# Two transformer blocks: pair transfers behind their forms, and twelve seven-product slabs in the first feed forward

## The chip, the cores and the metric

One NeuronCore of one Trainium2 chip runs the whole kernel. The time is the device time of one execution in microseconds; the median of several runs is what counts. One more execution was taken with the profiler on, and all rows below come from it.

## The reference

256 tokens of width 1024, all in float32, go through two blocks. What matters here is the end of the first block, its feed forward:

```
u = rmsnorm(h, norm_ff_g) @ w1          # 1024 -> 4096
h = h + square(relu(u)) @ w2            # 4096 -> 1024
```

The first block has in front of it a mixer (`w_in`, softmax attention with forget gates, a gated recurrence, `w_out`) and cross attention over 256 memory tokens. The second block (differential attention, pooling, memory attention, gates, a convolved feed forward) follows it. The kernel computes float32 products in three passes of TensorE: each operand is split into a high part (`hi`, fp32r) and the remainder (`lo`), and `mm3` issues hi x hi, hi x lo and lo x hi.

## The kernel before

**Slabs.** All weights stream through a ring of three buffers (`RING = 3`) as slabs of up to 128 x 2048 elements, numbered through the whole kernel in the order of use. SyncE (SP) loads slab n into `raw` (`load`) once the low part of slab n-3 has been made. ScalarE makes `whi` (`hi`), once slab n-3 has left TensorE. VectorE makes `wlo` (`lo`), and TensorE multiplies.

**First feed forward.** `w1` is cut in 16 up slabs `u0` to `u15` (256 hidden columns each), `w2` in 16 down slabs (256 hidden rows each). `FIRST_FFN` is the order, written out by hand: `u` is an up slab, `n` a plain down slab (8 block products of 128 x 128 with 512 columns, 24 matmuls), and `s` a down slab by seven products of blocks (Strassen and Winograd's scheme, 21 matmuls). HIDS = 7 places hold the split hidden activations between an up slab and its down slab.

**What a seven-product slab needs.** Three of its seven products use blocks of the slab as loaded; four use forms T1 to T4, sums and differences of blocks:

- T1 and T3 are made by transfers. SP loads two blocks of the upper half into `pairs` (`pair`, line 523), and GpSimd then adds the other two by an accumulating DMA into the same place (`add_blocks`, line 738). `pairs` has two buffers, `forms_hi`/`forms_lo` one (`FORMS = 1`).
- The three blocks that are used as they are (in `raw`; in the text, "the forms of n" on SP) come by two transfers: line 534 (512 KB) and line 535 (256 KB).
- T2 and T4 are made by VectorE in `rest` (`weight_sums`, lines 2440 and 2441), which waits for the accumulate's semaphore `sev["acc0"]` or `sev["acc1"]`.
- ScalarE makes `forms_hi` (`form_hi`, line 1825) and VectorE `forms_lo` (`form_lo`, line 2448), each in two halves; `sev["lo"]` counts the halves. TensorE waits for the first half after nine matmuls and for the second after fifteen (`seven_slab`).
- The hidden side needs sums too: `hidden_sums` (lines 2417 to 2420, tile `sq`) before `hid_hi` (line 1813) and `hid_lo` (line 2426).

**Order on VectorE.** For position n of the order: `hidden_sums` if it is an up slab for a seven-product slab; `form_lo` twice for a slab whose forms buffer comes free with n; `lo(n + 3)`; `weight_sums(n + 3)` if that is a seven-product slab; `hidden_lo`. ScalarE goes the same way with `relu_square`, `form_hi`, `hi(n + 3)`, `hidden_hi`. `split_after` says at which position a slab's forms are split: when slab n-3 is done or the seven-product slab before it, whichever is later.

**Pair transfers before.** `load(n)` issues, right behind slab n's own transfer, the pair of slab n+2 if that is a seven-product slab. It counts on the semaphore of slab n (`raw_landed`), so ScalarE's `hi(n)` waits for it as well. From the third pair on, SP waits first until the first half of `forms_lo` of the slab two seven-product slabs back is made, since the buffer is used again. `add_blocks` on GpSimd waits for slab n-2's semaphore.

Of the kernel before, what the change touches and what calls it, by code (L numbers as in the profile page):

```python
# [35 lines left out]
RING = 3  # L36
HIDS = 7
FORMS = 1
SQUARES = 2
FIRST_FFN = "u0 u1 u2 u3 u4 u5 u6 s0 u7 s1 u8 s2 u9 s3 u10 s4 u11 s5 u12 s6 u13 s8 u14 s10 u15 n7 s12 n9 s14 n11 n13 n15"  # L40
SLAB = 2048
NEG = -1e30
EPS = 1e-6
# [7 lines left out]
def ffn_order():  # L51

    return [(step[0], int(step[1:])) for step in FIRST_FFN.split()]

# [69 lines left out]
def two_blocks(nc, w, out):  # L124
# [4 lines left out]
    slabs, first = plan(w)  # L129
# [13 lines left out]
    SEVEN = [n0 + i for i, (kind, j) in enumerate(ORDER) if kind == "s"]  # L143
# [2 lines left out]

    landed = [0] * NS
    for n in range(NS):
        landed[n] = (landed[n - RING] if n >= RING else 0) + (32 if n in SEVEN or n >= first["cv"] else 16) + 16 * (n + 2 in SEVEN)

    with ExitStack() as ctx:
        def sem(name):
            return ctx.enter_context(nc.semaphore(name))

        def sb(name, shape, dt=F32, at=None):
            return (at or ctx).enter_context(nc.sbuf_tensor(name, shape, dt))

        def sems(prefix, names):
            return {n: sem(f"{prefix}_{n}") for n in names.split()}
# [55 lines left out]
        with ExitStack() as r3:  # L215
# [4 lines left out]
            pairs = sb("pairs", [P, 2, 2, 512], at=r3)  # L220
# [48 lines left out]
        raw_landed = [sem(f"raw_landed{i}") for i in range(RING)]  # L269
# [8 lines left out]
        lam_in, bias_in, mem_in = (sem(n) for n in "lam_in bias_in mem_in".split())  # L278
# [26 lines left out]
        sev = sems("sev", "acc0 acc1 t hi lo kept")  # L305
# [59 lines left out]
        def slab(t, n, nk):  # L365
            return t[:, n % RING, :nk * slabs[n][3]].rearrange("p (k c) -> p k c", k=nk)
# [73 lines left out]
        def quarter(t, q, order=QUARTERS):  # L440
            tt, c = order[q]
            return t[:, tt, c * 512:c * 512 + 512]
# [27 lines left out]
            return out  # L470

        EARLY = SEVEN[0] - first["w1"]

        def up_bank(j):

            return tb[:, j - 1, :] if j in (2, 3, 4) else acc[:, 0, 0, :] if j == 5 else acc[:, 1, 1, :]
# [5 lines left out]
        held, places, before = {}, {}, {}  # L482
# [22 lines left out]
        def raw_forms(n):  # L505
            return raw[:, n % RING, :].rearrange("p (s c) -> p s c", c=512)
# [7 lines left out]
        @block.sync  # L514
        def _(sp):
            def pair(n):

                if n + 2 not in SEVEN:
                    return
                i = SEVEN.index(n + 2)  # L520
                if i >= 2:
                    sp.wait_ge(sev["lo"], 2 * i - 3)
                sp.dma_start(pairs[:, i % 2, :, :], slabs[n + 2][1][:, :, 512:1024]).then_inc(raw_landed[n % RING], 16)

            def load(n, src=None, wait=None):
                if n >= RING:

                    sp.wait_ge(lo_ready, n - RING + 1 if wait is None else wait)
                if n - RING in SEVEN:
                    sp.wait_ge(sev["t"], SEVEN.index(n - RING) + 1)  # L530
                _, ap, nk, c, _ = slabs[n]
                if n in SEVEN:
                    forms = raw_forms(n)
                    sp.dma_start(forms[:, 1:3, :], ap[:, :, 0:512]).then_inc(raw_landed[n % RING], 16)
                    sp.dma_start(forms[:, 3, :], ap[:, 1, 512:1024]).then_inc(raw_landed[n % RING], 16)
                    pair(n)
                    return
                dst, src = slab(raw, n, nk), ap if src is None else src
                if n < first["cv"]:
                    sp.dma_start(dst, src).then_inc(raw_landed[n % RING], 16)  # L540
                    pair(n)
                    return

                for part in range(2):
                    if len(src.shape) == 4:
                        d, s = dst[:, :, part * P:part * P + P], src[:, :, part, :]
                    else:
                        d, s = dst[:, part, :], src[:, part, :]
                    sp.dma_start(d, s).then_inc(raw_landed[n % RING], 16)

            def loop(name, src, iters):

                n0 = first[name]
                with sp.Fori(0, iters) as i:
                    for u in range(RING):
                        load(n0 + u, src(i, u), i * RING + (n0 + u - RING + 1))

            def load_x(q):
                t, c = QUARTERS[q]
                sp.dma_start(quarter(h, q), w["x"][t * P:t * P + P, c * 512:c * 512 + 512]).then_inc(x_in[q], 16)  # L560

            def load_piece(n, p):

                _, ap, nk, _, _ = slabs[n]
                if n >= RING and p == 0:
                    sp.wait_ge(lo_ready, n - RING + 1)
                w = nk // PIECES[n]
                k = slice(p * w, p * w + w)
                landed_at = raw_landed[n % RING] if p == PIECES[n] - 1 else piece_in[n % RING, p]
                sp.dma_start(slab(raw, n, nk)[:, k, :], ap[:, k, :]).then_inc(landed_at, 16)  # L570

            for g in range(4):
                sp.dma_start(turned_x[:, 2 * g:2 * g + 2, :], w["xT"][:, 2 * g:2 * g + 2, :]).then_inc(xT_in[g], 16)
                load_piece(0, g)
                load_piece(1, g)
            for p in range(PIECES[2]):
                load_piece(2, p)
            for q in range(4):
                load_x(q)
            for p in range(PIECES[RING]):  # L580
                load_piece(RING, p)
            sp.dma_start(cols[:, 16:NC0 + NCW], w["cols"][:, 16:NC0 + NCW]).then_inc(cols_in["rest"], 16)
            sp.dma_start(small[0:8, 59:60], w["fox_f_bias"].rearrange("a h -> h a"),
                         allow_slow_non_contiguous=True).then_inc(bias_in, 16)
            for i, n in enumerate(("lambda_q1_2", "lambda_k1_2", "lambda_q2_2", "lambda_k2_2")):
                sp.dma_start(fpt[:, 0, 64 * i:64 * i + 64], w[n].broadcast_to([P, 64])).then_inc(lam_in, 16)
            for n in range(RING + 1, first["cv"]):
                if n in PIECES:
                    for p in range(PIECES[n]):
                        load_piece(n, p)  # L590
                else:
                    load(n)
            upv = w["w_up_2"].rearrange("(k p) (two c) -> p k two c", p=P, two=2)
            loop("cv", lambda i, u: upv[:, :, :, bass.ds(i * 384 + u * 128, 128)], 7)
            for n in range(first["cv"] + 21, NS):
                load(n)
# [3 lines left out]
        def _(pool):  # L600
# [79 lines left out]
            for m in range(1, 8):  # L680

                half = 1 << (m - 1)
                n = P // (2 * half)
# [48 lines left out]
            def add_blocks(n):  # L732

                i = SEVEN.index(n)
                pool.wait_ge(raw_landed[(n - 2) % RING], landed[n - 2])
                if i >= 2:
                    pool.wait_ge(sev["lo"], 2 * i - 3)
                pool.dma_start(pairs[:, i % 2, :, :], slabs[n][1][:, 0, :].rearrange("p (a c) -> p a c", a=2),  # L738
                               accum_op=ALU.add).then_inc(sev[f"acc{i % 2}"], 16)

            add_blocks(SEVEN[0])
            square_scale()

            pool.dma_start(xn[:, 1, :], w["final_norm_g"].rearrange("(a c) -> a c", a=1).broadcast_to([P, D])
                           ).then_inc(gfin_in, 16)
            for n in SEVEN[1:]:
                add_blocks(n)
# [19 lines left out]
            for g, win in enumerate(POOL_W):  # L767
# [5 lines left out]
                n = win - 1  # L773
# [2034 lines left out]
```

## Time and profile before

| | us |
|---|---|
| median of 3 runs | 883.44 (882.94 to 883.51) |
| profiled execution | 884.5 |
| its span | 882.8 |
| TensorE busy | 872.9 (99%) |
| VectorE busy | 648.7 (73%) |
| ScalarE busy | 521.2 (59%) |
| granted TensorE clock | 0.999 |

The span is what the profiler shows from the first to the last instruction; the rest of the profiled execution's time lies around it. The first feed forward lies between about 269 and 443 us of the span. In the page and the views, PE is TensorE, DVE is VectorE, ACT is ScalarE, POOL is GpSimd and SP is SyncE; `L798` is a line of the kernel. Matmuls overlap in the pipeline, so the distance between two starts says more than the duration shown.

### The profile page before, as it was taken

Reading aid. Unit: us, or ns where it says so; the run is one execution under the profiler, and the core shown is the slowest. Engines: PE = TensorE matmul, PEld = TensorE weight load, DVE = VectorE, ACT = ScalarE, POOL = GpSimd, SP = SyncE. Lnnn points to the kernel's source line nnn. Section 1 sums busy time; section 2 is a strip of 40 time slices with the busy share of each in tenths; the row PEclk is TensorE's granted clock in tenths of the full one; section 3 lists DMA queues with packets and bytes.
Section 4 is the critical chain, followed back from the end, with each engine's and each line's share of the span. In section 5 each row is a group of like instructions: output and inputs, shape, how many; then the busy total and the mean of one; then the engine's idle time right before and its main releaser. Section 6 shows DMA issues by size and latency. Waiting matters only on the chain.

```text
span 882.8 us, 15682 instructions
## 1 busy us (share of the span) xinstructions
PE 872.9 (99%) x6254; PEld 806.4 (91%) x6254; DVE 648.7 (73%) x887; ACT 521.2 (59%) x761; POOL 127.8 (14%) x147
## 2 busy tenths in 40 slices
PE   9999999999999999999999999999999999999997
PEld 9998988989989998888899989999998899999886
DVE  5887987757538888897875548988686788888643
ACT  6786655546547766675573356656634766666432
POOL 5561333000000100000142250001000100000000
PEclk9999999999999999999999999999999999999999
DMA  9969544354535989998656554354556387676541
GB/s 296 319 232 299 178 144 144 97 174 150 176 92 183 254 239 261 268 296 268 203 175 220 192 186 141 106 190 137 174 192 191 104 226 195 194 196 204 192 143 48
DMA packets 141932, 169.42 MB, mean 192 GB/s; under 512 B 4592, under 2 KB 114288, under 8 KB 141616
## 3 DMA queue, kind: packets, MB, share of 16 engines
q1 hardware_dynamic: 138224, 155.72, 55.0%
q0 software_dynamic: 2928, 11.80, 5.5%
q8 instruction: 43, 0.70, 0.4%
q10 hardware_dynamic: 720, 1.06, 0.3%
q14 instruction: 17, 0.14, 0.1%
HBM read 167.51 MB, written 1.05 MB: 191 GB/s over the span
## 4 chain that ended last, share of the span: by engine, by line
PE 85%; DVE 5%; DMA 4%; issue 3%; ACT 2%; SPq 0%; POOL 0%; DVEq 0%; POOLq 0%; ACTq 0%
PE tb L798 15%; PE tb L800 15%; PE tb L799 15%; PE acc L798 10%; PE acc L800 10%; PE acc L799 10%; DMA pairs<-in_w 3%; DMA raw<-in_w_in 1%; PE acc L1140 1%; DVE forms_lo L2448 1%; ACT whi L1487 1%; DVE hid_lo L2426 1%; DVE wlo L2054 1%; DVE rest L2440 1%; DVE wlo L2127 1%
## 5 line engine op out<-in xcount | busy, mean ns | idle before, releaser
L2054 DVE TENSOR_TENSOR wlo<-raw,whi 128x2048 fp32r<-128x2048 f32 (+1 forms) x138 | 310.4, 2254 | 126.2 <-ACT whi L1487 125.5
L1487 ACT ACTIVATE whi<-raw 128x2048 fp32r<-128x2048 f32 (+1 forms) x138 | 259.3, 1880 | 151.7 <-PE acc L800 79.3
L798 PE MATMUL tb<-xhi,whi 128*128 128x256 f32 x1000 | 278.7, 279 | 0.8 <-DVE wlo L2127 0.5
L799 PE MATMUL tb<-xlo,whi 128*128 128x256 f32 x1000 | 276.4, 276 | 0.0
L800 PE MATMUL tb<-xhi,wlo 128*128 128x256 f32 x1000 | 276.3, 276 | 0.0
L798 PEld LDWEIGHTS tb<-xhi,whi 128*128 128x128 f32 x1000 | 187.9, 188 | 1.9 <-issue 1.8
L799 PEld LDWEIGHTS tb<-xlo,whi 128*128 128x128 f32 x1000 | 187.9, 188 | 0.1
L800 PEld LDWEIGHTS tb<-xhi,wlo 128*128 128x128 f32 x1000 | 187.9, 188 | 0.0
L798 PE MATMUL acc<-xhi,whi 128*128 128x256 f32 x256 | 71.4, 279 | 1.0 <-DVE wlo L2054 1.0
L799 PE MATMUL acc<-xlo,whi 128*128 128x256 f32 x256 | 70.8, 277 | 0.0
L800 PE MATMUL acc<-xhi,wlo 128*128 128x256 f32 x256 | 70.8, 276 | 0.0
L798 PEld LDWEIGHTS acc<-xhi,whi 128*128 128x128 f32 x256 | 48.1, 188 | 2.9 <-issue 2.8
L799 PEld LDWEIGHTS acc<-xlo,whi 128*128 128x128 f32 x256 | 48.1, 188 | 0.2
L800 PEld LDWEIGHTS acc<-xhi,wlo 128*128 128x128 f32 x256 | 48.1, 188 | 0.0
L800 PE MATMUL acc<-whi,xlo 128*128 128x512 f32 x112 | 44.0, 393 | 0.0
L798 PE MATMUL acc<-whi,xhi 128*128 128x512 f32 x112 | 43.9, 392 | 0.0
L799 PE MATMUL acc<-wlo,xhi 128*128 128x512 f32 x112 | 43.8, 391 | 0.0
L2003 ACT ACTIVATE cy<-tb,cols 128x256 f32<-128x256 f32 x44 | 22.5, 561 | 33.1 <-PE tb L800 33.1
L791 POOL TENSOR_TENSOR rs<-rs,half_neg 128x1 f32<-128x1 f32 x6 | 3.3, 554 | 266.7 <-DVE rs L2665 266.7
L738 POOL DMA_DIRECT2D pairs<-in_w x11 | 9.6, 877 | 170.9 <-DMA pairs<-in_w 170.9
L799 PE MATMUL acc<-wlo,vhi 128*128 128x512 f32 x88 | 34.2, 389 | 0.0
L798 PE MATMUL acc<-whi,vhi 128*128 128x512 f32 x88 | 34.2, 389 | 0.0
(435 smaller groups left out, 1737.9 us busy)
## 6 DMA issues: line engine op xcount, KB each, us to landing
raw<-in_w_in SPq DMA_DIRECT2D x37, 1024.0 KB, 5.3
raw<-in_w_up SPq DMA_DIRECT2D x44, 512.0 KB, 5.0
raw<-in_w SPq DMA_DIRECT2D x21, 1024.0 KB, 6.5
raw<-in_w_down SPq DMA_DIRECT2D x22, 512.0 KB, 4.1
raw<-in_w_xkv SPq DMA_DIRECT2D x8, 1024.0 KB, 5.6
raw<-in_w_out SPq DMA_DIRECT2D x8, 1024.0 KB, 4.9
pairs<-in_w SPq DMA_DIRECT2D x11, 512.0 KB, 4.9
pairs<-in_w POOLq DMA_DIRECT2D x11, 512.0 KB, 7.9
```

The lines of the kernel that those rows point to most:

```text
L738: pool.dma_start(pairs[:, i % 2, :, :], slabs[n][1][:, 0, :].rearrange("p (a c) -> p a c", a=2), accum_op=ALU.add).then_inc(sev[f"acc{i % ...
L798: pe.matmul(o, a_hi, b_hi, start=start, stop=False)
L799: pe.matmul(o, a_hi, b_lo, start=False, stop=False)
L800: return pe.matmul(o, a_lo, b_hi, start=False, stop=stop)
L1140: last = pe.matmul(acc[:, 1, t, i * 64:i * 64 + 64], a[:, s], lvl_view(b[:, s], m)[:, :, 1, :], start=True, stop=True)
L1487: act.activation(whi[:, n % RING, cut], raw[:, n % RING, cut], ACT.Copy).then_inc(hi_ready, 1)
L2003: last = act.activation(cy[:, b, g, :], tb[:, b, g * T:g * T + T], ACT.Identity, scale=cols[:, bass.ds(j + a, 1)], bias=cols[:, bass.ds(j ...
L2054: dve.tensor_tensor(low(n)[:, cut], raw[:, n % RING, cut], whi[:, n % RING, cut].bitcast(F32), ALU.subtract).then_inc(lo_ready, 1)
L2127: dve.tensor_tensor(low(n)[:, cut], raw[:, n % RING, cut], whi[:, n % RING, cut].bitcast(F32), ALU.subtract)\
L2426: dve.tensor_tensor(hid_lo[:, cut], sq[:, j % SQUARES, 0:cut.stop - cut.start], hid_hi[:, cut].bitcast(F32), ALU.subtract).then_inc(ffn["l ...
L2440: link(dve.tensor_tensor(t2, t1, b22, ALU.add))
L2448: dve.tensor_tensor(forms_lo[:, i % FORMS, cut, :], src, forms_hi[:, i % FORMS, cut, :].bitcast(F32), ALU.subtract).then_inc(sev["lo"], 1)
```

## The change

- `PAIR_IN`: the pair transfers count on two semaphores of their own, `lam_in` for even and `bias_in` for odd ones (both have been used once at the start of the kernel, up to 64 and 16). `landed` no longer counts them, and `hi` no longer waits for them.
- `pair(n)` is now issued for slab n itself, behind its two form transfers, and no longer with slab n-2.
- `add_blocks(n)` waits for the pair's own semaphore, and no longer for `sev["lo"]`.
- `FIRST_FFN`: the seven-product slabs are 0 to 10 and 12 (before: 0 to 6, 8, 10, 12, 14), the plain ones 11, 13, 14 and 15 (before: 7, 9, 11, 13, 15). `s9` and `s10` stand side by side, and `n13 n14 n15` are the last three.

```diff
-FIRST_FFN = "u0 u1 u2 u3 u4 u5 u6 s0 u7 s1 u8 s2 u9 s3 u10 s4 u11 s5 u12 s6 u13 s8 u14 s10 u15 n7 s12 n9 s14 n11 n13 n15"
+FIRST_FFN = "u0 u1 u2 u3 u4 u5 u6 s0 u7 s1 u8 s2 u9 s3 u10 s4 u11 s5 u12 s6 u13 s7 u14 s8 u15 s9 s10 n11 s12 n13 n14 n15"
@@ plan of the landings
-        landed[n] = (landed[n - RING] if n >= RING else 0) + (32 if n in SEVEN or n >= first["cv"] else 16) + 16 * (n + 2 in SEVEN)
+        landed[n] = (landed[n - RING] if n >= RING else 0) + (32 if n in SEVEN or n >= first["cv"] else 16)
@@
+        PAIR_IN = ((lam_in, 64), (bias_in, 16))
@@ SP
             def pair(n):
 
-                if n + 2 not in SEVEN:
-                    return
-                i = SEVEN.index(n + 2)
+                i = SEVEN.index(n)
                 if i >= 2:
                     sp.wait_ge(sev["lo"], 2 * i - 3)
-                sp.dma_start(pairs[:, i % 2, :, :], slabs[n + 2][1][:, :, 512:1024]).then_inc(raw_landed[n % RING], 16)
+                sp.dma_start(pairs[:, i % 2, :, :], slabs[n][1][:, :, 512:1024]).then_inc(PAIR_IN[i % 2][0], 16)
@@ SP, load(n)
                 if n < first["cv"]:
                     sp.dma_start(dst, src).then_inc(raw_landed[n % RING], 16)
-                    pair(n)
                     return
@@ GpSimd
             def add_blocks(n):
 
                 i = SEVEN.index(n)
-                pool.wait_ge(raw_landed[(n - 2) % RING], landed[n - 2])
-                if i >= 2:
-                    pool.wait_ge(sev["lo"], 2 * i - 3)
+                landing, before = PAIR_IN[i % 2]
+                pool.wait_ge(landing, before + 16 + 16 * (i // 2))
                 pool.dma_start(pairs[:, i % 2, :, :], slabs[n][1][:, 0, :].rearrange("p (a c) -> p a c", a=2),
                                accum_op=ALU.add).then_inc(sev[f"acc{i % 2}"], 16)
```

## Rows read from the trace of the kernel before

**Rows 1.** The page's first part: busy time, share of the span, instructions.

```profile
PE 872.9 (99%) x6254; PEld 806.4 (91%) x6254; DVE 648.7 (73%) x887; ACT 521.2 (59%) x761; POOL 127.8 (14%) x147
```

**Rows 2.** Windows between starts of seven-product slabs: length, busy PE, PEld, DVE, ACT, POOL.

```profile
308.31:318.56 10.25, 10.25 (x72) 9.41 (x70) 10.08 (x13) 7.91 (x8) 0.86 (x1) 1.00 0.91 241
...
360.02:371.85 11.83, 10.82 (x72) 9.29 (x71) 9.67 (x9) 7.39 (x8) 0.86 (x1) 1.00 0.85 243
...
sum 95.24, PE 93.61 PEld 84.17 DVE 79.80 ACT 63.81 POOL 7.78; mean PE 10.40 PEld 9.35 DVE 8.87 ACT 7.09 POOL 0.86
```

**Rows 3.** Waits from 265 to 445 us: total, times, longest.

```profile
ACT whi L1487 <- DMA pairs<-in_w: 16.5, 7, 3.1
...
PEld tb L798 <- DVE forms_lo L2448: 1.3, 2, 1.0
PE acc L798 <- DVE wlo L2054: 1.0, 3, 0.4
```

**Rows 4.** Chain that ended last, one stretch: start, us, what.

```profile
362.82 3.85 DMA pairs<-in_w
366.69 1.50 ACT whi L1487
```

**Rows 5.** Timeline of TensorE, first matmuls of slabs: start, duration.

```profile
313.09 0.28 PE L798 MATMUL acc<-xhi,whi 128*128 128x256 f32 x1
...
398.07 0.28 PE L798 MATMUL acc<-xhi,whi 128*128 128x256 f32 x1
...
403.55 0.39 PE L798 MATMUL acc<-whi,hid_hi 128*128 128x512 f32 x1
...
423.96 0.39 PE L798 MATMUL acc<-whi,hid_hi 128*128 128x512 f32 x1
```

**Rows 6.** Timeline of VectorE, one cycle.

```profile
332.98 0.28 DVE L2417 TENSOR_TENSOR sq<-sq 128x128 f32<-128x128 f32 x1
...
335.37 1.76 DVE L2054 TENSOR_TENSOR wlo<-raw,whi 128x1536 fp32r<-128x1536 f32 x1 [1.24 <-ACT whi L1487]
337.04 0.68 DVE L2440 TENSOR_TENSOR rest<-pairs,raw 128x512 f32<-128x512 f32 x1
337.76 0.69 DVE L2441 TENSOR_TENSOR rest<-rest,raw 128x512 f32<-128x512 f32 x1
338.37 1.08 DVE L2426 TENSOR_TENSOR hid_lo<-sq,hid_hi 128x896 fp32r<-128x896 f32 x1
339.49 1.23 DVE L2448 TENSOR_TENSOR forms_lo<-pairs,forms_hi 128x1024 fp32r<-128x1024 f32 x1
340.63 1.22 DVE L2448 TENSOR_TENSOR forms_lo<-rest,forms_hi 128x1024 fp32r<-128x1024 f32 x1
341.77 2.28 DVE L2054 TENSOR_TENSOR wlo<-raw,whi 128x2048 fp32r<-128x2048 f32 x1
```

**Rows 7.** Timeline of SP's issues: start, duration.

```profile
289.56 0.55 SPq L523 DMA_DIRECT2D pairs<-in_w  x1
...
333.10 0.37 SPq L534 DMA_DIRECT2D raw<-in_w  x1
333.51 0.47 SPq L535 DMA_DIRECT2D raw<-in_w  x1
```

**Rows 8.** Line 523, the pair transfers: issue durations in ns, landing in us.

```profile
L523 SPq DMA_DIRECT2D pairs<-in_w x11: 367/368/789, 278.1 to 392.5; - x11
...
DMA to landing us min/median/max: 3.7/4.9/8.5
```

**Rows 9.** Line 535, the 256 KB transfer behind the 512 KB one.

```profile
L535 SPq DMA_DIRECT2D raw<-in_w x11: 458/468/1904, 287.6 to 399.6; - x11
...
DMA to landing us min/median/max: 5.5/6.8/9.8
```

**Rows 10.** Line 738, the accumulating transfers of GpSimd.

```profile
L738 POOL DMA_DIRECT2D pairs<-in_w x11: 863/865/965, 286.5 to 400.9; - x11
...
DMA to landing us min/median/max: 6.9/7.9/9.5
```

## The prediction

> **What bounds the kernel now.** I read the page's busy shares first: TensorE is busy for 99% of the span [rows 1], so a change counts only by what it takes from TensorE's stream or by the time that it makes TensorE wait. Then the windows, cut at the starts of the first feed forward's seven-product slabs. Nine cycles of one seven-product slab and one up slab take 95.24 us; the undisturbed ones take 10.25 us, the worst 11.83 [rows 2]. Nine times 10.25 is 92.25, so TensorE loses 3.0 us there. The third reading is the list of waits in the stage: TensorE waits for `forms_lo` and `wlo`, which VectorE makes, and ScalarE waits 16.5 us, in seven waits, for the DMA of `pairs` before it may split a slab [rows 3]. The chain of waits shows this as a closed circle: pair DMA issued at 362.82, split by ScalarE at 366.69 [rows 4]; the sums, the low halves and the next pair DMA follow. So the stage is paced by a loop through the pair transfer, just above TensorE's own pace. The slab that waits is the one loaded together with the pair, two slabs ahead of the pair's own user, because both count on one semaphore.
>
> **TensorE's own work.** The window from 308.31 is cut by the first up product at 313.09 [rows 2, 5]: a seven-product slab (21 matmuls) takes 4.78 us, an up slab 5.47. A plain slab has 24 matmuls, by the same pitch 24 x 4.78 / 21 = 5.46. Twelve seven-product slabs in place of eleven save 0.68 us of the stream.
>
> **VectorE's work for it.** Slabs 7 and 9 become seven-product slabs, 14 no longer is one: each gives or takes four `sq` operations like the one of 0.28 us (1.2 with their gaps, the next work in the queue starts no sooner) and a `hid_lo` of seven blocks for one of four (1.08 x 3/7 = 0.4), 1.6 us in all [rows 6], plus forms and sums for one slab net. A cycle with all of it fits: the first window holds 10.08 us of VectorE work and TensorE still kept 10.25 [rows 2, 6]. I cost that at nothing as long as no wait is put in VectorE's queue; the bounds are nothing and the 1.6 us of each of the two, since VectorE has no more than 0.2 us to spare in such a cycle.
>
> **The transfers, which decide.** Removed: ScalarE's wait on the pair of two slabs ahead (up to the 3.0 us above come back), and SP's wait for `sev["lo"]` in front of the up slab's load. Under the new order that wait is met before it is reached, since `pair(n)` now stands behind the forms of slab n itself. Added: the pair's lead over its user shrinks by two slabs. For seven-product slab n the order is now:
>
> 1. SP issues the forms of n when `wlo` of slab n-3, an up slab, is done. Two issues at 333.10 and 333.51 with 0.47 us for the second [rows 7]: the pair goes out 0.9 us later. That assumes that nothing holds the issue.
> 2. The pair lands. The trace has no pair that follows its forms at the usual distance. Bounds: 3.7 us (a pair alone ahead in the queue) and 8.5 (the slowest one) [rows 8]. The nearest row is that of the 256 KB forms transfer, which stands at the end of SP's pair of form transfers: 5.5 / 6.8 / 9.8 us [rows 9]. I take 6.8.
> 3. GpSimd sees it and issues the accumulating DMA: 0.3 us from the wake-up, my estimate from GpSimd's issue lying a little behind ScalarE's start on the same landing. It lands after 6.9 / 7.9 / 9.5 us [rows 10]. I take 7.9.
> 4. VectorE, whose queue stands at `weight_sums(n)` until then, does both `rest` sums, `hid_lo`, `forms_lo` twice and `wlo` of the up slab n+1: from 337.04 to 341.77 + 2.28 = 344.05, that is 7.0 us [rows 6].
> 5. The end of that `wlo` is what releases the forms of slab n+4.
>
> This is a loop over four slabs, that is over two cycles: 0.9 + 6.8 + 0.3 + 7.9 + 7.0 = 22.9 us. TensorE needs 2 x 10.25 = 20.5. So the loop binds: 11.45 us per cycle. It binds as soon as pair and accumulate together take over 20.5 - 8.2 = 12.3 us; I have 14.7.
>
> The Trainium skill has a rule that bears on step 2 (DMA: Bandwidth & Descriptors, section "Queues, rings and completion order"): each DMA engine takes its descriptors in ring order within a queue and takes turns between queues. By it a pair behind 768 KB of forms lands after them and shares the engines with GpSimd's transfer. The spread of the pair's landings here, 3.7 to 8.5 us, fits this but doesn't show the order; my sum does not use it.
>
> **Start of the stage.** The pair of the first seven-product slab goes out behind its forms at 288.1 to 289.6 (L523 issues at 289.56 there now, for the next pair) instead of 278.1 [rows 7, 8]. With 7 to 8 us for the pair and 7.9 for the accumulate its sum is ready at 303.5 to 306. Behind it in VectorE's queue stand the sums (1.35), `hid_lo` (1.1), both `forms_lo` (2.3), four `sq` operations (1.2) and then `wlo` of the up slab (2.2) that TensorE wants at 313.09: 8.15 us [rows 6]. With the middle, 305, that is 313.1, no loss; the bounds are 0 and 1.1 us. From there VectorE has no lead, and each `wlo` of an up slab starts that slab.
>
> From the up slab 7 at 313.1 to up slab 15 there are eight cycles, four turns of the loop: 4 x 22.9 = 91.6, so slab 15 starts at 404.7. Before, it starts at 398.07 [rows 5]. **Loss: 6.6 us** (the 3.0 that come back are inside this difference).
>
> **The adjacent slabs.** There is one buffer of forms, so forms of s10 can be split only when s9 has ended. TensorE has nine matmuls of s10 that need none, 9 x 0.228 = 2.05 us; ScalarE (1.05) and VectorE (1.2) need 2.3 to 2.4. That alone is a stall of 0.3 us. But VectorE is late. The forms of s9 follow `wlo` of slab 14, which belongs to the other turn of the loop. That one starts with `wlo` of slab 8: behind 313.1 come `hid_lo`, four `sq`, `wlo` of a seven-product slab (1.7), sums, `hid_lo`, both `forms_lo` and `wlo`, 11.0 us, so 324.1, and three turns later 392.8. Plus 0.9 + 6.8 + 0.3 + 7.9, s9's accumulate lands at 408.7, sums and `hid_lo` to 410.7, both `forms_lo` to 413.0, `wlo` of s10 to 414.7. It then stands at the sums of s10, whose pair waited for the first `forms_lo` of s8 (404.7 - 7.0 + 1.35 + 1.1 + 1.15 = 401.3) and so lands with 6.8 + 0.3 + 7.9 at 416.3. Sums to 417.7, `wlo` of n11 to 419.9, `hid_lo` of slab 15 to 420.6, first `forms_lo` of s10 to 421.7. TensorE: slab 15 from 404.7 to 410.2, s9 to 415.0, the nine matmuls to 417.05. **Stall: 4.65 us.** Bounds 0.3 and 6. The rest (n11, s12, n13, n14, n15) has its splits in time by the same counting, as the plain slabs before have (no stall after 403.55), and the fold and residual are unchanged.
>
> **Sum.** 6.6 + 4.65 - 0.68 = 10.6 us. Before, n11 starts at 423.96; the slab that takes its place (n13) should start near 434.6. The profiled execution took 884.5 us with a span of 882.8; 1.7 us lie around it. The median of the runs is 883.44, 1.1 under the profiled one. I add the difference to the median: 894.0 us.
>
> **Rivals.**
>
> A, forecast: the loop through pair and accumulate binds. Between loops of 21.8 (pair 5.7) and 24.5 (both some 0.8 longer) and a stall of s10 of 2.5 to 6: 888 to 900 us. Chance 0.60.
>
> B, the landings get shorter when the pair's burst is spread out, pair 5.2 with 7.9: loop 21.3, as much as now (4 x 21.3 = 85.2 against 84.98), and VectorE instead of the transfers is what paces the rest. Stall of s10 some 2: 883.44 + 0.2 + 2 - 0.7 = 884.9. For it: half of the pair transfers before land within 4.9 us [rows 8]. Against: these lead their burst in the queue. Chance 0.15, from 883 to 888.
>
> C, the other side: pair and accumulate take under 12.3 us together, TensorE has its own pace. Then the 3.0 us come back, 0.68 are saved, and s10 costs 0.3 to 1: 880.2. One mechanism, decided at 12.3; the lowest rows (3.7 and 6.9) would allow it, the medians behind other transfers (6.8 and 7.9) speak against it. Chance 0.17. The skill's fit in the same page, section "Anatomy of one DMA — SWDGE (gpsimd) path", about 2 us plus bytes over 436 GB/s, would give 3.2 us for 512 KB, both together 6.4, and hence this result; no accumulate here landed under 6.9 [rows 10], so the trace speaks against it.
>
> D, both at their long ends through contention (8.5 and 9.5): loop 26.2, 4 x 26.2 = 104.8, a loss of 20 and 5 at s10: 907. Slower cycles thin the traffic, which speaks against it. Chance 0.08.
>
> **Chances.** What a measurement can tell from no change is 0.2%, 1.8 us. Faster by more: nearly all of C, 0.16. Within: the bottom of B and the edge of C, 0.08. Slower: 0.76. Range 881 to 900; the forecast's own is 888 to 900.
>
> **What the profile after would show.** Right: VectorE's idle time stands before `rest` L2440, released by the DMA of `pairs`; ScalarE's wait of `whi` on `pairs` is gone; windows between up slabs 7 and 15 come in twos of about 23 us; accumulate issues 7 us behind their pair; TensorE has one stall of 3 to 5 us in front of a `forms_hi` product near the end. Wrong: `rest` waits for nothing, cycles of 10.25 to 10.3, the 3.0 us gone; or a pair landing under 5 us behind its forms. If the stage is slower and `rest` waits for no DMA, VectorE's own work was mis-sized.

## The result, and the profile after

| | before | after |
|---|---|---|
| median, us (22 runs each) | 883.71 | 887.04 |
| lowest to highest | 881.51 to 886.35 | 882.83 to 889.41 |
| span of the profiled execution | 882.8 | 885.0 |

The ratio is 1.0033, interval 1.0024 to 1.0042: the change makes the kernel slower by 3.3 us. The forecast was 894.0, slower by 10.6. The direction was right, the size was wrong by a factor of three. The profiled span grew by 2.2 us; the parts below are counted against that.

TensorE's line of the page, where [rows 1] stands for before:

```profile
PE 873.0 (99%) x6251; PEld 807.1 (91%) x6251; DVE 652.6 (74%) x895; ACT 523.2 (59%) x763; POOL 125.0 (14%) x148
```

Three matmuls fewer, as counted. The windows of the stage, cut at the starts of seven-product slabs and around the late stalls; columns as in [rows 2], the third number from the end is the granted clock:

```profile
307.88:318.13 10.25, 10.25 (x71) 9.42 (x70) 9.89 (x12) 7.91 (x8) 0.85 (x1) 1.00 0.88 251
...
379.61:390.42 10.81, 10.52 (x72) 9.32 (x70) 9.59 (x9) 7.94 (x9) 0.85 (x1) 1.00 0.96 275
390.42:400.66 10.24, 10.24 (x71) 9.41 (x70) 5.57 (x4) 4.50 (x5) 1.71 (x2) 1.00 0.94 260
400.66:404.87 4.21, 2.22 (x11) 1.51 (x9) 3.26 (x5) 2.88 (x3) 0.00 (x0) 1.00 0.89 207
...
405.90:409.08 3.18, 3.18 (x8) 2.46 (x8) 3.15 (x5) 3.02 (x4) 0.00 (x0) 0.50 0.77 258
409.08:413.07 3.99, 2.48 (x12) 1.69 (x10) 3.96 (x4) 3.38 (x3) 0.86 (x1) 1.00 0.68 211
```

Of the nine cycles up to s9, eight take 10.24 or 10.25 us and one 10.81. From 307.88 to 400.66 are 92.8 us, against 95.2 before. What the change loses against before lies behind 400.66, in s9 and s10. The waits between 265 and 447 us (total, times, longest), where [rows 3] stands for before:

```profile
ACT forms_hi L1822 <- DMA pairs<-in_w: 27.8, 10, 6.6
DVE rest L2437 <- DMA pairs<-in_w: 16.1, 10, 5.3
...
PEld tb L795 <- DVE forms_lo L2445: 4.4, 2, 2.4
...
PE acc L795 <- DVE wlo L2051: 0.3, 1, 0.3
```

ScalarE's wait of `whi` on `pairs` is gone. VectorE's `rest` now waits for the accumulate in ten of twelve slabs. Both are signs that the forecast named for being right. But the cycles of 10.25 us and the 3.0 us gone are signs that it named for being wrong. One turn of the loop in the timelines of SP, GpSimd and VectorE (start, duration):

```profile
331.19 0.37 SPq L533 DMA_DIRECT2D raw<-in_w  x1
...
332.11 0.43 SPq L522 DMA_DIRECT2D pairs<-in_w  x1
...
352.39 0.37 SPq L533 DMA_DIRECT2D raw<-in_w  x1
```

```profile
338.46 0.85 POOL L735 DMA_DIRECT2D pairs<-in_w  x1 [10.01 <-DMA pairs<-in_w]
```

```profile
345.35 0.69 DVE L2437 TENSOR_TENSOR rest<-pairs,raw 128x512 f32<-128x512 f32 x1 [0.80 <-DMA pairs<-in_w]
...
350.08 2.28 DVE L2051 TENSOR_TENSOR wlo<-raw,whi 128x2048 fp32r<-128x2048 f32 x1
```

Forms issued at 331.19, pair 0.9 later, accumulate issued 6.35 after the pair, `rest` 6.9 after that, `wlo` ends at 352.36, and SP issues the forms four slabs further at 352.39: 21.2 us, against the 22.9 of the forecast and TensorE's 20.5. Landings of the pair on SP (the view of the tile `pairs`, SP alone) and of the accumulate (line 735), min / median / max, beside [rows 8] and [rows 10]. The trace tells the landing of only six of the twelve pairs; over all twelve, the accumulate's issue stands 4.8 to 8.6 us behind the pair's, 6.15 in the median.

```profile
DMA to landing us min/median/max: 5.3/6.1/8.3
```

```profile
L735 POOL DMA_DIRECT2D pairs<-in_w x12: 846/855/959, 294.4 to 409.6; - x12
...
DMA to landing us min/median/max: 5.5/7.3/9.5
```

How far VectorE is ahead of TensorE: the `wlo` of the up slabs 7 and 15, and the first matmul of each:

```profile
307.33 2.28 DVE L2051 TENSOR_TENSOR wlo<-raw,whi 128x2048 fp32r<-128x2048 f32 x1
...
391.95 2.29 DVE L2051 TENSOR_TENSOR wlo<-raw,whi 128x2048 fp32r<-128x2048 f32 x1
```

```profile
312.66 0.28 PE L795 MATMUL acc<-xhi,whi 128*128 128x256 f32 x1
...
395.19 0.28 PE L795 MATMUL acc<-xhi,whi 128*128 128x256 f32 x1
```

The end of the stage in the chain that ended last (start, length, what):

```profile
369.51 8.20 DMA pairs<-in_w
377.73 0.70 DVE rest L2437
...
382.54 2.21 DVE wlo L2051
...
385.74 5.95 DMA pairs<-in_w
...
391.98 9.54 DMA pairs<-in_w
401.54 0.70 DVE rest L2437
...
411.79 1.24 DVE forms_lo L2445
413.07 0.50 PE tb L795
```

This is the loop itself, closed through the split that releases the load: s7's accumulate (8.2 us), `wlo`, s9's pair (6.0), s9's accumulate (9.5). TensorE at the same place, and the first product of n13:

```profile
404.87 0.50 PE L795 MATMUL tb<-forms_hi,hid_hi 128*128 128x512 f32 x1 [1.99 <-DVE forms_lo L2445]
...
405.69 0.63 PE L795 MATMUL tb<-forms_hi,hid_hi 128*128 128x512 f32 x1
406.12 0.63 PE L796 MATMUL tb<-forms_lo,hid_hi 128*128 128x512 f32 x1
...
426.12 0.39 PE L795 MATMUL acc<-whi,hid_hi 128*128 128x512 f32 x1
```

s9 waits 2.15 us beyond the usual pitch for its first form (2.38 between two starts). Then the matmuls stand 0.43 us apart where 0.23 is usual, from 405.69 to 409.08, while the granted clock is 0.50, which is 1.2 instead of 2.4 GHz: eight steps in 3.39 us, 1.6 us lost. s10 waits 1.67 more. With 0.5 in the cycle of 379.61 that is 5.9 us lost (6.1 with the first matmul behind each stall, which takes 0.1 longer); regained are the 3.0 of the loop before and the 0.68. The difference is 2.2 to 2.4, as n13's start says (426.12 against 423.96 for the slab in that place, [rows 5]).

### The profile page after: what moved, and what is told of

The parts are those of the page before. It is cut to its first block, busy times and chain, and to the rows that moved or that the text cites. A ratio compares the mean times of both kernels' runs of the same rounds, so it can differ in the third digit from the quotient of the medians.

```text
span 885.0 us, 15677 instructions
## 1 busy us (share of the span) xinstructions
PE 873.0 (99%) x6251; PEld 807.1 (91%) x6251; DVE 652.6 (74%) x895; ACT 523.2 (59%) x763; POOL 125.0 (14%) x148
## 4 chain that ended last, share of the span: by engine, by line
PE 82%; DMA 9%; DVE 6%; issue 1%; ACT 1%; SPq 1%; POOL 0%; DVEq 0%; POOLq 0%; ACTq 0%
PE tb L795 15%; PE tb L797 15%; PE tb L796 15%; PE acc L795 10%; PE acc L797 10%; PE acc L796 9%; DMA pairs<-in_w 8%; DVE forms_lo L2445 1%; DVE wlo L2051 1%; PE acc L1137 1%; DMA raw<-in_w_in 1%; DVE wlo L2124 1%; DVE hid_lo L2423 1%; DVE rest L2437 0%; PE tb L1337 0%
## 5 line engine op out<-in xcount | busy, mean ns | idle before, releaser
L2051 DVE TENSOR_TENSOR wlo<-raw,whi 128x2048 fp32r<-128x2048 f32 (+1 forms) x138 | 309.6, 2248 | 108.4 <-ACT whi L1484 107.8
```

Source lines behind the costliest of these rows:

```text
L2051: dve.tensor_tensor(low(n)[:, cut], raw[:, n % RING, cut], whi[:, n % RING, cut].bitcast(F32), ALU.subtract).then_inc(lo_ready, 1)
```

## The experiments

All times are medians, compared with runs of the kernel before on the same chip; the ratio stands with its 95% interval. The two parts of the change were first taken apart.

**e1, the new order alone.**

```diff
 (kernel before)
-FIRST_FFN = "... u13 s8 u14 s10 u15 n7 s12 n9 s14 n11 n13 n15"
+FIRST_FFN = "... u13 s7 u14 s8 u15 s9 s10 n11 s12 n13 n14 n15"
```

> The new order alone; pair transfers as before (two slabs ahead, on the slab's semaphore). Theory A (the loop through the pair and the accumulate, 21.2 us per two cycles in the changed kernel's trace, makes the forms of the late slabs late; the adjacent slabs only add to it): the 3.0 us lost by the loop of before stay, 0.7 saved, 0.3 to 1.5 for s10 behind s9: 883.0 to 884.6, no clear difference from before. Rival R1 (the adjacency of s9 and s10 alone makes the loss): 886 to 887. Rival R2 (the later pair transfers alone make it): 882.7 to 883.2.

Measured: 896.38, ratio 1.0128 (1.0111 to 1.0146), 12.4 us slower. None of the theories had that. SP's issues and TensorE (timelines):

```profile
385.48 0.41 SPq L540 DMA_DIRECT2D raw<-in_w  x1
396.31 0.37 SPq L523 DMA_DIRECT2D pairs<-in_w  x1
396.72 0.47 SPq L534 DMA_DIRECT2D raw<-in_w  x1
```

```profile
404.30 0.55 PE L798 MATMUL acc<-xhi,whi 128*128 128x256 f32 x1 [4.95 <-DVE wlo L2054]
...
422.16 0.79 PE L798 MATMUL tb<-forms_hi,hid_hi 128*128 128x512 f32 x1 [3.51 <-DVE forms_lo L2448]
```

Two slabs ahead, the pair of s10 stands in SP's queue behind the load of slab 15 and in front of the forms of s9, and waits for its buffer until the first `forms_lo` of s8 is made (396.28). For 10 us SP issues nothing. That pair also counts on the semaphore of slab 15, whose own load went out at 385.48, so ScalarE's split of slab 15 waits for it, and with it `wlo` and TensorE's first stall, 5.1 us. At s10 it is the same with the pair of s12, issued at 409.36: 3.7 us. ScalarE's two splits:

```profile
399.92 1.91 ACT L1487 ACTIVATE whi<-raw 128x2048 fp32r<-128x2048 f32 x1 [4.34 <-DMA pairs<-in_w]
...
412.93 1.49 ACT L1487 ACTIVATE whi<-raw 128x1536 fp32r<-128x1536 f32 x1 [4.30 <-DMA pairs<-in_w]
```

With adjacent slabs two pairs follow each other closer than the two buffers allow, and the shared semaphore hands that wait on to ScalarE.

**e2, the later pair transfers alone.**

```diff
 (changed kernel)
-FIRST_FFN = "... u13 s7 u14 s8 u15 s9 s10 n11 s12 n13 n14 n15"
+FIRST_FFN = "... u13 s8 u14 s10 u15 n7 s12 n9 s14 n11 n13 n15"
```

> The new pair transfers alone, old order (11 seven-product slabs, none adjacent, fewer of them late). Theory A: most of the 3.0 us come back, since each turn of the loop (21.2 us) is only 0.7 us over TensorE's 20.5 and the lead at the start covers that; the late slabs give 0 to 1.5 back: 881 to 882.5. Rival R1: 880.5 to 881. Rival R2: 885.5 to 887.

Measured: 884.68, ratio 1.0008 (0.9994 to 1.0023), no clear difference. Theory A had 881 to 882.5, R1 less and R2 more than what was measured. In the profiled execution, nine cycles lose 2.6 us, so hardly any of the 3.0 comes back: TensorE is late in every second cycle (around 344.12, 365.35 and 386.87, by 0.7 to 1.0 us each), and one place shows another queue:

```profile
408.31 0.50 PE L795 MATMUL acc<-whi,hid_hi 128*128 128x512 f32 x1 [1.40 <-ACT ru L1792]
```

ScalarE, which waits for the accumulate in front of `forms_hi`, is late to empty up slab 15. So the later pair by itself costs about what ScalarE's wait on the pair did before.

**e3, the changed kernel with no two adjacent.**

```diff
-... u15 s9 s10 n11 s12 n13 n14 n15
+... u15 s9 n11 s10 n13 s12 n14 n15
```

> The changed kernel with s10 and n11 exchanged and s12 and n13 exchanged (u15 s9 n11 s10 n13 s12 n14 n15), so that twelve seven-product slabs stay and none are adjacent. Theory A: the stall of s10 (1.7 us) goes, that of s9 (2.2 us in the changed kernel's trace, and the 1.8 us at half clock behind it) shrinks only as far as s9's accumulate meets less traffic: 882.5 to 885. Rival R1: all of the loss and more goes, 880 to 881. Rival R2: no change from the changed kernel, 886 to 887.

Measured: 887.28, ratio 1.0038 (1.0025 to 1.0051), as the changed kernel and not the 882.5 to 885 of theory A. The two stalls at s9 and s10 are gone in its profile; other ones came: 1.0 us at 362.19, 0.7 at two more slabs, and one that the order itself makes:

```profile
435.72 0.39 PE L797 MATMUL acc<-whi,hid_lo 128*128 128x512 f32 x1
438.86 0.33 PE L950 MATMUL tb<-ident,h 128*128 128x128 f32 x1 [2.74 <-DVE h L2091]
```

With two plain slabs behind the last seven-product slab, VectorE's fold of the products (432.5 to 438.0) isn't done when the residual is wanted. Two plain slabs at the end are too few in this order. So this run can't price the adjacency.

**e4, own semaphores, pairs two slabs ahead again, new order.**

```diff
 (changed kernel, pair)
+                if n not in SEVEN:
+                    return
 (load of a seven-product slab n)
-                    pair(n)
+                    pair(n + 2)
 (load of another slab n of this part)
+                    pair(n + 2)
```

> The changed kernel, with the pair issued two slabs ahead again as before the change, but on its own semaphores (ScalarE's split does not wait for it), new order. Theory A: no loop through the accumulate, 3.0 us come back but for what SP's wait in front of the up slabs' loads costs, 0.7 saved, 0.3 to 1.5 for s10: 880.5 to 882.5. Rival R1: 884 to 886 (the adjacency stays). Rival R2: 880 to 881.

Measured: 888.62, ratio 1.0051 (1.0038 to 1.0064). That is slower than any of the three expectations. Nine cycles of 10.25 without one stall, then 6.2 us at s10, and half clock behind it:

```profile
413.33 0.80 PE L798 MATMUL tb<-forms_hi,hid_hi 128*128 128x512 f32 x1 [6.02 <-DVE forms_lo L2448]
```

```profile
400.41 0.37 SPq L524 DMA_DIRECT2D pairs<-in_w  x1
400.82 0.47 SPq L541 DMA_DIRECT2D raw<-in_w  x1
```

SP's part of e1's cause is left: the pair of s12 waits at SP for `forms_lo` of s9, and the load of n11 behind it starts at 400.82; ScalarE waits 5 us for n11 with the forms of s10 behind it in its queue. Against e1 this run has only the semaphores of its own, and it is 7.8 us faster.

**e10, own semaphores and nothing else: pairs two slabs ahead, old order.** The edit of e4 on the order of before; against the kernel before, its main line is the one below, with `PAIR_IN`, `landed` and the waits of `add_blocks` as in the change.

```diff
 (kernel before)
-                sp.dma_start(pairs[:, i % 2, :, :], slabs[n + 2][1][:, :, 512:1024]).then_inc(raw_landed[n % RING], 16)
+                sp.dma_start(pairs[:, i % 2, :, :], slabs[n + 2][1][:, :, 512:1024]).then_inc(PAIR_IN[i % 2][0], 16)
```

> The kernel before with one thing taken from the change: the pair transfers count on their own semaphores and ScalarE's split no longer waits for them; they stay two slabs ahead, the order is the old one. Theory A (late pairs make the loop; ScalarE's wait on them was what cost before): all nine cycles at TensorE's 10.25 us, 3.0 us back: 880.5 to 881.5. Rival (own semaphores gain nothing, since SP's wait in front of the up slabs' loads takes the place of ScalarE's): 883 to 885.

Measured: 881.03, ratio 0.9972 (0.9962 to 0.9982), faster than both. A window as long as nine cycles of 10.25 us, with TensorE busy in all of it:

```profile
307.80:400.05 92.25, 92.25 (x623) 84.75 (x622) 82.65 (x84) 65.09 (x64) 7.77 (x9) 1.00 0.96 282
```

The 3.0 us are back: before, it was ScalarE's wait that cost them, and SP's wait costs nothing in the old order.

**e12, new order, the pairs of s10 and s12 behind their forms, the others two slabs ahead.**

```diff
 (changed kernel, pair, now pair(n, late=False))
+                if n not in SEVEN or late != (SEVEN.index(n) >= 10):
+                    return
 (load of a seven-product slab n)
-                    pair(n)
+                    pair(n, late=True)
+                    pair(n + 2)
 (load of another slab n of this part)
+                    pair(n + 2)
```

> New order, own semaphores; pairs two slabs ahead for s0 to s9, and only those of s10 and s12 behind their own forms, so that SP does not hold the loads of s9, n11 and s12 behind a pair that waits for its buffer. Theory A with the adjacency priced at 0.3 to 1.5: 3.0 and 0.7 back, 880.1 to 882. Rival R3 (at the adjacent slabs VectorE's queue is what is late, whatever the transfers do): s10 stalls by 2 or more, 883 to 885.

Measured: 881.06, ratio 0.9971 (0.9960 to 0.9981). As e10. At the late slabs SP is held for no more than 0.9 us, and the adjacency shows its own price:

```profile
407.76 0.50 PE L799 MATMUL tb<-forms_hi,hid_hi 128*128 128x512 f32 x1 [0.58 <-DVE forms_lo L2449]
```

0.74 us between the starts beyond the pitch and 0.1 in the next matmul. That is about the 0.68 us that the twelfth slab saves.

**e5, the pair in front of its two form transfers.**

```diff
 (changed kernel, load of a seven-product slab n)
+                    pair(n)
                     sp.dma_start(forms[:, 1:3, :], ...)
                     sp.dma_start(forms[:, 3, :], ...)
-                    pair(n)
```

> The changed kernel with the pair issued in front of its two form transfers and no longer behind them. Theory A: the pair lands 1 to 1.5 us earlier relative to the slab's load (0.9 us of issue and its place in the queue), the loop drops from 21.2 to 22.5 to about 20 to 21, s9's forms are ready 1 to 3 us earlier: 883.5 to 885.5. Rival (the accumulate and not the pair's place in the queue sets it): 886.5 to 887.5.

Measured: 885.94, ratio 1.0023 (1.0008 to 1.0037). By the medians 1.1 us better than the changed kernel, but the two intervals overlap, and 885.94 lies between the two expectations (up to 885.5, from 886.5), so this run decides neither. The pair lands in 5.5 instead of 6.1 us, for the six pairs whose landing each trace tells, the accumulate in 7.9 instead of 7.3 (the first row is the pair's, the second the accumulate's):

```profile
DMA to landing us min/median/max: 3.7/5.5/6.4
```

```profile
DMA to landing us min/median/max: 5.2/7.9/9.1
```

What the one wins, the other gives back in part. The profiled execution, one of the shorter ones (span 881.8), shows s10 alone late, by 3.0 us.

**e6, no accumulate.** The products with T1 and T3, and all that follows from them, lack the blocks that it adds.

```diff
-                pool.dma_start(pairs[...], ..., accum_op=ALU.add).then_inc(sev[f"acc{i % 2}"], 16)
+                pool.sem_inc(sev[f"acc{i % 2}"], 16)
```

> The changed kernel without GpSimd's accumulating DMA (the forms T1 and T3 then lack the blocks that it adds); GpSimd raises the same semaphore as soon as the pair has landed. Theory A: 6.9 to 9.5 us leave each turn of the loop, it can't bind; only the adjacency's own price stays (forms of s10 split after s9: 0.3 to 1.5): 880.1 to 881.5. If the adjacency is costly by itself (rival R1): 883 or more.

Measured: 881.12, ratio 0.9968 (0.9958 to 0.9979): the whole loss of the changed kernel and the loss of before are gone, though order and place of the pairs are those of the changed kernel. Nine cycles take 92.22 us, and one stall is left, the adjacency's, 0.7 us as in e12:

```profile
407.66 0.50 PE L794 MATMUL tb<-forms_hi,hid_hi 128*128 128x512 f32 x1 [0.53 <-DVE forms_lo L2444]
```

The kernel also moves 0.5 MB less per seven-product slab, so this run doesn't tell whether it is the time of the accumulate in the loop or its traffic that costs.

**e13, the first accumulate later.** The forecast had its sum at 305; in the changed kernel the sums start at 301.56 and wait for nothing.

```diff
 (changed kernel, GpSimd)
+            pool.wait_ge(ffn["lo"], 4)
             add_blocks(SEVEN[0])
```

> The changed kernel with one wait more: GpSimd starts the first accumulate only when the low half of hidden slab 3 is made (near 298.2 us of the span, 3.7 us later than the 294.45 of the changed kernel), so that its sum lands at about 305.3, as the prediction had it, and the first sums wait. Theory A (the loop is 0.4 to 0.5 us a cycle slower than TensorE and the lead at the start hides that): with 3.1 us of lead taken away TensorE stalls several times between up slabs 7 and 15 and the whole is 2.5 to 4 us slower than the changed kernel, 889.5 to 891.5. Rival (the loss arises at the late slabs alone, the early lead is worth nothing): 886.5 to 887.5.

Measured: 891.92, ratio 1.0098 (1.0081 to 1.0115), 8.2 us over before and, over two sets of runs, 4.9 over the changed kernel, just above what theory A had. The way isn't the one I expected. The accumulate took 9.4 us, the sum came at 307.6, 6.0 later than in the changed kernel and not the 3.7 that I aimed at, and TensorE lost its time at once:

```profile
310.66 0.57 PE L796 MATMUL tb<-whi,hid_hi 128*128 128x512 f32 x1 [2.85 <-ACT ru L1793]
311.03 0.63 PE L797 MATMUL tb<-wlo,hid_hi 128*128 128x512 f32 x1
```

ScalarE stood at `forms_hi` with the emptying of an up slab behind it. TensorE waited 2.9 us, ran at a granted clock of 0.51 from 311.0 to 314.4, and then lost only 1 us in the next eight cycles: the stall had made the lead anew. At s10 it lost 3.1 us and had the half clock again, in all nearly what the late slabs cost the changed kernel. So a start 6.0 us later costs TensorE 2.9 us and the clock behind it, which fits a lead of about 3 us. What the loop would cost without a lead, this run doesn't show.

## Why the prediction was right or wrong

**TensorE's own work, right.** Three matmuls fewer; cycles of 10.25.

**VectorE's work at nothing, right.** e6 has all of it and keeps 92.22 us over nine cycles.

**ScalarE's wait costs 3.0 us before, right.** e10 takes it away alone and gains 2.6 us by the medians.

**The loop, right in kind; its length, 22.9 us, is the step that failed.** It goes through the steps as listed, and the step of VectorE (7.0) and of SP (0.9) came out to the tenth. The two transfers were sized too long. In the turn shown, step 2 and GpSimd's 0.3 took 6.35 us where I had 7.1, and step 3 took 6.9 where I had 7.9; the medians of the landings are 6.1 and 7.3, where I had 6.8 and 7.9. That is 21.2 us a turn. From the end of `wlo` of slab 7 (309.61) to that of slab 15 (394.24) VectorE takes 84.6 us for four turns, not 91.6. TensorE goes from slab 7 to slab 15 in 82.5 us (312.66 to 395.19), 9.1 less than forecast, and 7.0 of the 9.1 are this term. With 21.2 the forecast's own sum puts slab 15 at 397.9, just ahead of the 398.07 of before, and with the rest left as it was the change would cost 3.8 us and not 10.6. So most of the miss in size is here.

I took the pair from the 256 KB forms transfer of before. That one itself fell from 6.8 to 5.0 us in the median, as its line now shows. Before, an accumulate was issued within a microsecond of it in seven of eleven cases; that this is the reason is likely, not shown.

```profile
L534 SPq DMA_DIRECT2D raw<-in_w x12: 341/468/1619, 287.2 to 403.4; - x12
...
DMA to landing us min/median/max: 4.0/5.0/7.6
```

A row that was measured beside traffic which the change moves away bounds a term, it doesn't size it. e5's pair lands after 5.5 us in front of the forms and after 6.1 behind them. The rule of the Trainium skill on ring order (DMA: Bandwidth & Descriptors, "Queues, rings and completion order") fits this. The Trainium skill's fit on the same page, "Anatomy of one DMA — SWDGE (gpsimd) path", gives an estimate of 3.2 us for 512 KB. It is stated for transfers that GpSimd issues, so rival C should not have used it for SP's pair. For the accumulate the traces disagree with it: none landed under 5.2 us (e5, e13).

**"No loss; ... from there VectorE has no lead", wrong, by the same two terms.** For the first sum I had 7 to 8 us for the pair and 7.9 for the accumulate. The first pair was issued at 288.81 and its accumulate at 294.45, 5.6 us later, and the accumulate landed in 7.1 or less. The sums were on time, and the up slab that I had at 313.1 was split at 309.6, when TensorE wanted it at 312.66. That is 3.05 us of lead. Four turns use up the 84.6 - 82.0 = 2.6 us by which VectorE is slower than TensorE's own 4 x 20.5, and TensorE itself loses 0.5 at slab 14, so at slab 15 VectorE is still 0.95 ahead (394.24 and 395.19). The 2.1 us of lead that went are the rest of the 9.1. Slab 15 starts at 395.19 (forecast 404.7, before 398.07).

**Rival B.** It had a loop of 21.3 us and a time from 883 to 888, and 887.04 lies there. Its mechanism isn't what the trace shows: it had the pair at 5.2 us, VectorE as what paces the rest, and 2 us at s10.

**The adjacent slabs, right in size by luck, wrong in parts.** Forecast 4.65 at s10; measured 2.15 at s9, 1.6 by the clock and 1.67 at s10, 5.4 in all. The forecast had no stall at s9 and built s10's on the loop of 22.9. s9's accumulate took 9.5 us (I had 7.9): s10's forms, pair and accumulate (397.15) and n11's load ran beside it. The half clock behind a stall was not in my sum. Nor is SP's wait for the buffer always met before it is reached: the pairs of s10 and s12 go out 1.4 us behind their forms' second issue and not 0.5 (390.84 and 404.85). The adjacency's bare price, 0.3 in the forecast, is 0.8 in e6 and e12.

**What e1 shows the forecast missed.** I costed the order and the pairs together, from a working in which the pair stands behind its forms. That the new order can't stand with the pairs of before I had not seen: alone it costs 12.4 us. Semaphores of their own give 7.8 of that back (e4), the later pairs with them 9.1 (the changed kernel), and moving only the two pairs of s10 and s12 all of it and 2.6 more (e12). In the sum that changed nothing.

**Open.** How much of the accumulate's 7 to 9 us is its own and how much the traffic beside it; why e3 is as slow as the changed kernel beyond the 2.9 us at its end and the stalls of its one profiled execution.

## What to carry to other kernels

When a transfer chain is moved closer to its user, close the loop through the buffers, and write beside its excess per turn the lead with which the stage enters it: here 2.6 us of excess in four turns were covered by 3.05 us of lead. A transfer that nobody needs yet shouldn't count on a semaphore that somebody waits for now, and a wait for its buffer shouldn't stand in an in-order queue in front of loads that are needed sooner. The two fastest versions that compute everything take the semaphores of their own from the change: in the old order with all pairs left two slabs ahead (e10, 881.03), or in the new order with only the pairs of s10 and s12 moved behind their forms (e12, 881.06).

## What the runs showed of the hardware that wasn't expected

- A stall of TensorE can cost more than itself. With the stalls of 2.15 us (changed kernel), 2.9 and 3.1 (e13), 3.7 and 5.1 (e1) and 6.2 (e4) the granted clock fell to 0.50, in the long ones before the stall had ended, and 3 to 4 us of TensorE's work behind them ran at it, with 0.43 us from matmul to matmul for 0.23. With 1.67 (changed kernel), 1.6 (e2), 2.9 (e3) and 3.0 (e5) it stayed at 1.00. So the length of the stall alone doesn't tell whether the clock falls.
- The spread of the runs went with the slack of the pair and the accumulate, though no run tests this as a cause. Where TensorE waits at the end of their chain, runs of one kernel lie 5 to 7 us apart (changed kernel 882.8 to 889.4, e5 883.0 to 889.1, e2 882.0 to 888.3, before 881.5 to 886.4); where it doesn't, 0.7 to 2.2 (e6 880.8 to 881.4, e12 880.9 to 881.7, e10 880.7 to 882.9). e1, e3, e4 and e13, with four to eight runs each, have 1.1 to 4.0 us from lowest to highest.
